# Feed-forward gate-and-up chunks taken in pairs: high-weight products of both, then low-weight products of both

## The chip, the cores and the metric

One core of one Trainium2 chip runs the whole program. The metric is the device time of one execution in microseconds (us), as the median over several executions.

## What is computed

Two DeepNorm layers over 256 tokens of width 1024 in float32. Each layer is a mixer (layer 0: sparse attention and stick-breaking attention; layer 1: block attention) followed by a SwiGLU feed-forward of width 2816. Only the feed-forwards are touched here:

```python
D_FF = -(-8 * D_MODEL // (3 * 256)) * 256      # 2816
def swiglu(x, w_gate, w_up, w_down):
    return (jax.nn.silu(x @ w_gate) * (x @ w_up)) @ w_down

def reference(...):
    for i in range(DEPTH):                     # DEPTH = 2
        ...                                    # mixer and layer norm
        f = swiglu(h, ffn_gate[i], ffn_up[i], ffn_down[i])
        h = layer_norm(DEEPNORM_ALPHA * h + f, ln_ffn_g[i], ln_ffn_b[i])
```

## The kernel before

**Products in parts.** Each float32 weight and activation is split into a high part (rounded to the matmul format fp32r) and a low part (the remainder), and a product is high x high + high x low + low x high. For the gate and up projections the activations lie as `hTs[:, k]`, high and low side by side, 512 columns. `half_hi` runs 8 matmuls of 512 columns, one for each 128 rows of the contraction, with the high weights `whi`; this makes the high x high sum in columns 0 to 255 of a PSUM bank and the high x low sum in columns 256 to 511. `half_lo` adds 8 matmuls of 256 columns with the low weights `wlo` to columns 0 to 255. One **tile** is 128 columns of gate and the same 128 of up: two banks, 16 wide and 16 narrow matmuls.

**The weight stream.** All weights come in chunks of 1 MB, in halves of 512 KB, into two raw buffers (`RAW` = 2). ScalarE (ACT) casts a half to `whi` (`split_hi`, L367), VectorE (DVE) subtracts to get `wlo` (`split_lo`, L737), both into a ring of six chunks (`RING` = 6), four chunks ahead of use (`AHEAD` = 4). The DMA for a half, issued by SyncE (SP, L287), waits until DVE has finished with the same half two chunks earlier. A cast into a ring slot waits until TensorE (PE) has used the chunk that lies in it (`chunk_used`).

**The feed-forward.** A layer has 22 tiles. Tiles 0 and 1 are computed by rows, tiles 2 and 3 one after the other. Then eight **groups** follow, each with three chunks: a down chunk (24 matmuls, L1212, function `out_chunk`) for two earlier tiles, and two gate-and-up chunks. PE writes out the first two groups and loops over the other six; ACT and DVE loop over all eight (`LOOPS` = 4, two groups in each turn). Tiles 20 and 21 come after the last group with no down chunk ahead of them, then the last three down chunks and the layer norm. Banks 4 to 7 accumulate the down products. An even tile has banks 2 and 3, an odd one banks 0 and 1, so a tile's first matmul waits until the tile two before it has been read out (`usum_ready`).

**Reading out a tile** (`ffn_tile`) goes back and forth between ACT and DVE: ACT copies the gate's high x low half (L632), DVE adds (L1016), ACT takes silu (L635) and copies the up half (L637), DVE adds (L1019, after which both banks are free) and multiplies (L1024), ACT casts (L639), DVE subtracts (L1027). The last two make `ahi` and `alo`, which a later down chunk reads.

Each engine runs its instructions in the order in which they are written; semaphores alone couple the engines.

Of the kernel before, what the change touches and what calls it, by code (L numbers as in the profile page):

```python
# [43 lines left out]
AHEAD = 4  # L44
# [16 lines left out]
def build(nc, x, xT, stream, w_uk, w_uv, kv_norm, ln_rows, consts, out):  # L61
    with ExitStack() as ctx:
# [198 lines left out]
        def tile_bank(t):  # L261

            return 2 * ((t + 1) % 2)
# [100 lines left out]
        def _(act):  # L364
# [5 lines left out]
            def split_hi(c, i=0):  # L370

                if c >= RING or not isinstance(i, int):
                    act.wait_ge(chunk_used, c - RING + 1 + RING * i)
                for j in range(2):
                    split_hi_half(c, j, i)
# [249 lines left out]
            def ffn_tile(L, c, t, i=0, more=1, ahi_first=False):  # L625

                n = FT * L + t + 4 * i
                m = n + 1 - 2 * (L + 1)
                if more and not ahi_first:
                    split_hi(c + AHEAD, i)  # L630
                act.wait_ge(gate_done, m)
                nc.scalar.copy(gful[:, t % 2], bank[tile_bank(t)][:, S:2 * S]).then_inc(glo_ready, 1)  # L632
                act.wait_ge(gsum_ready, m)
                act.wait_ge(amul_ready, n - 1)
                nc.scalar.activation(sgate[:, t % 2], gful[:, t % 2], ACT.Silu).then_inc(silu_ready, 1)  # L635
                act.wait_ge(chunk_used, c + 1 + RING * i)
                nc.scalar.copy(uful[:, t % 2], bank[tile_bank(t) + 1][:, S:2 * S]).then_inc(ulo_ready, 1)  # L637
                act.wait_ge(amul_ready, n + 1)
                nc.scalar.copy(ahi[:, FF_SLOT[t], :], aful[:, t % 2]).then_inc(ahi_ready, 1)  # L639
                if more and ahi_first:  # L640
                    split_hi(c + AHEAD, i)

            def ffn(L):


                base = L0_FFN if L == 0 else L1_FFN
                ffn_rows(L, base)
                for t in (2, 3):
                    ffn_tile(L, base + t, t)
                with act.Fori(0, LOOPS) as i:  # L650
                    for j in range(2):
                        c = base + 4 + 3 * j
                        split_hi(c + AHEAD, i)
                        ffn_tile(L, c + 1, 4 + 2 * j, i)
                        ffn_tile(L, c + 2, 5 + 2 * j, i)
                c = base + 4 + RING * LOOPS
                for at in range(3):
                    more = c + at + AHEAD < CHUNKS
                    if at < 2:
                        ffn_tile(L, c + at, 4 + 4 * LOOPS + at, 0, more, at == 1)  # L660
                    elif more:
                        split_hi(c + at + AHEAD)
# [70 lines left out]
        def _(dve):  # L733
# [6 lines left out]
            def split_lo(c, i=0):  # L740

                for j in range(2):
                    split_lo_half(c, j, i)
# [266 lines left out]
            def ffn_tile(L, c, t, i=0, more=1, alo_first=False):  # L1010
                n = FT * L + t + 4 * i
                m = n + 1 - 2 * (L + 1)
                if more and not alo_first:
                    split_lo(c + AHEAD, i)
                dve.wait_ge(glo_ready, m)
                nc.vector.tensor_tensor(gful[:, t % 2], bank[tile_bank(t)][:, 0:S], gful[:, t % 2], ALU.add  # L1016
                                        ).then_inc(gsum_ready, 1)
                dve.wait_ge(ulo_ready, m)
                nc.vector.tensor_tensor(uful[:, t % 2], bank[tile_bank(t) + 1][:, 0:S], uful[:, t % 2], ALU.add  # L1019
                                        ).then_inc(usum_ready, 1)  # L1020
                dve.wait_ge(silu_ready, n + 1)
                dve.wait_ge(usum_ready, m)
                dve.wait_ge(alo_ready, n - 1)
                nc.vector.tensor_tensor(aful[:, t % 2], sgate[:, t % 2], uful[:, t % 2], ALU.mult  # L1024
                                        ).then_inc(amul_ready, 1)
                dve.wait_ge(ahi_ready, n + 1)
                nc.vector.tensor_tensor(alo[:, FF_SLOT[t], :], aful[:, t % 2], ahi[:, FF_SLOT[t], :].bitcast(F32),  # L1027
                                        ALU.subtract).then_inc(alo_ready, 1)
                if more and alo_first:
                    split_lo(c + AHEAD, i)  # L1030

            def ffn(L):


                base = L0_FFN if L == 0 else L1_FFN
                ffn_rows(L, base)
                for t in (2, 3):
                    ffn_tile(L, base + t, t)
                with dve.Fori(0, LOOPS) as i:
                    for j in range(2):  # L1040
                        c = base + 4 + 3 * j
                        split_lo(c + AHEAD, i)
                        ffn_tile(L, c + 1, 4 + 2 * j, i)
                        ffn_tile(L, c + 2, 5 + 2 * j, i)
                c = base + 4 + RING * LOOPS
                for at in range(3):
                    more = c + at + AHEAD < CHUNKS
                    if at < 2:
                        ffn_tile(L, c + at, 4 + 4 * LOOPS + at, 0, more, at == 1)
                    elif more:  # L1050
                        split_lo(c + at + AHEAD)
# [46 lines left out]
        def _(pe):  # L1098
# [4 lines left out]
            def chunk(c, i=0):  # L1103
                pe.wait_ge(wlo_ready, 2 * c + 2 * RING * i)
# [12 lines left out]
            def half_hi(dst, slot, off):  # L1117

                for k in range(KT):
                    mm(dst[:], whi[:, slot, off + k * P:off + (k + 1) * P],  # L1120
                       hTs[:, k].rearrange("p j s -> p (j s)"), start=(k == 0), stop=False)
# [430 lines left out]
                                               aful[:, tile, t * P:(t + 1) * P], ident)  # L1552
                last.then_inc(ff_turned, 1)

            def gate_up(L, c, t, i=0):

                n = FT * L + t + 4 * i
                chunk(c, i)

                pe.wait_ge(usum_ready, n - 1 - 2 * (L + 1))  # L1560
                for half in range(2):
                    half_hi(bank[tile_bank(t) + half], c % RING, half * KT * P)
                half_lo(bank[tile_bank(t)], c % RING, 0).then_inc(gate_done, 1)
                half_lo(bank[tile_bank(t) + 1], c % RING, KT * P).then_inc(chunk_used, 1)

            def down(L, c, p, i=0, start=False):

# [4 lines left out]
            def ffn(L, n):  # L1572
                base = L0_FFN if L == 0 else L1_FFN

                chunk(base + 1)
                two = slice(base % RING, base % RING + 2)
                rows_wide(2 * L + 1, 0, two, bank[0][:], turn=n).then_inc(rows_done, 1)
                rows_wide(2 * L + 1, 1, two, bank[1][:]).then_inc(chunk_used, 2)

                def four_tiles(i, first=False):  # L1580
                    for j in range(2):
                        c = base + 4 + 3 * j
                        down(L, c, j, i, first and j == 0)
                        gate_up(L, c + 1, 4 + 2 * j, i)
                        gate_up(L, c + 2, 5 + 2 * j, i)

                chunk(base + 2)
                for half in range(2):
                    half_hi(bank[tile_bank(2) + half], (base + 2) % RING, half * KT * P)
                turn_rows(L, 0)  # L1590
                turn_rows(L, 1)
                half_lo(bank[tile_bank(2)], (base + 2) % RING, 0).then_inc(gate_done, 1)
                half_lo(bank[tile_bank(2) + 1], (base + 2) % RING, KT * P).then_inc(chunk_used, 1)
                chunk(base + 3)
                for half in range(2):
                    half_hi(bank[tile_bank(3) + half], (base + 3) % RING, half * KT * P)
                half_lo(bank[tile_bank(3)], (base + 3) % RING, 0).then_inc(gate_done, 1)
                half_lo(bank[tile_bank(3) + 1], (base + 3) % RING, KT * P).then_inc(chunk_used, 1)
                four_tiles(0, first=True)
                with pe.Fori(1, LOOPS) as i:  # L1600
                    four_tiles(i)
                c, p = base + 4 + RING * LOOPS, 2 * LOOPS
                gate_up(L, c, 2 * p + 4)
                gate_up(L, c + 1, 2 * p + 5)
                last_out([(c + 2 + j, FF_SLOT[2 * (p + j):2 * (p + j) + 2], FT * L + 2 * (p + j) + 2)
                          for j in range(3)], n + 1)
# [216 lines left out]
```

## Time and profile before

| | |
|---|---|
| median of 3 runs | 600.74 us (600.45 to 601.2) |
| the profiled execution, its own time | 599.96 us |
| its span in the trace | 598.2 us |
| PE matmul busy | 590.4 us (99%) |
| DVE busy | 422.7 us (71%) |
| ACT busy | 342.9 us (57%) |
| bytes read from HBM | 107.94 MB, 182 GB/s over the span |

The span runs from the first to the last instruction of the core. A matmul's recorded duration overlaps the next one's, so what counts for PE is the distance between starts. "Idle before" is time in which an engine stood still ahead of an instruction, with the engine whose event ended it.

### The profile page before, as it was taken

How to read it: one execution, taken by the hardware profiler on the slowest of the kernel's cores; microseconds unless marked ns; L12 is line 12 of the kernel's file. 1: busy time of each engine (PE TensorE's matmuls, PEld its weight loads, DVE VectorE, ACT ScalarE, POOL GpSimd, SP SyncE). 2: the span in 40 equal slices, each digit the busy share in tenths (PEclk: the TensorE clock that was granted, in tenths of full speed). 3: DMA queues.
4: the chain of work that ended last, by engine and by line, in shares of the span. 5: the costliest groups of instructions: out<-in, count | busy, mean ns of one | idle time of the engine just before them, and what ended most of it. 6: DMA issues, size and time to landing. Idle time of an engine off the chain costs nothing.

```text
span 598.2 us, 9656 instructions
## 1 busy us (share of the span) xinstructions
PE 590.4 (99%) x3387; PEld 508.1 (85%) x3387; DVE 422.7 (71%) x694; ACT 342.9 (57%) x644; POOL 27.3 (5%) x49
## 2 busy tenths in 40 slices
PE   9999999999999999999999999999999999999995
PEld 7988887888888888888888898888888888888885
DVE  4699868877776556655887878768677666665637
ACT  5777977466555544554556667636566455555430
POOL 1011111100000000000010000002000000000000
PEclk9999999999999999999999999999999999999999
DMA  8757427376765565564447543662767655555401
GB/s 312 264 178 263 141 70 250 104 253 215 233 219 187 196 204 180 182 205 140 146 139 273 184 141 112 210 202 77 236 217 239 213 189 170 181 188 192 140 1 70
DMA packets 30112, 109.43 MB, mean 183 GB/s; under 512 B 3376, under 2 KB 3376, under 8 KB 29952
## 3 DMA queue, kind: packets, MB, share of 16 engines
q1 hardware_dynamic: 28512, 102.77, 52.2%
q0 software_dynamic: 1568, 6.23, 3.1%
q8 instruction: 21, 0.34, 0.2%
q14 instruction: 11, 0.09, 0.0%
HBM read 107.94 MB, written 1.05 MB: 182 GB/s over the span
## 4 chain that ended last, share of the span: by engine, by line
PE 95%; DMA 2%; DVE 1%; ACT 1%; DVEq 0%; issue 0%; POOL 0%; ACTq 0%; POOLq 0%
PE bank L1212 27%; PE bank L1120 24%; PE bank L1126 13%; PE bank L1647 4%; PE bank L1476 3%; PE bank L1113 2%; PE bank L1190 2%; PE bank L1641 2%; PE bank L1651 2%; DMA raw<-stream_in 2%; PE bank L1166 2%; PE bank L1165 2%; PE bank L1172 2%; PE bank L1307 1%; PE bank L1318 1%; PE bank L1298 1%
## 5 line engine op out<-in xcount | busy, mean ns | idle before, releaser
L737 DVE TENSOR_TENSOR wlo<-raw,whi 128x1024 fp32r<-128x1024 f32 x190 | 225.0, 1223 | 44.0 <-ACT whi L367 43.7
L367 ACT CAST whi<-raw 128x1024 fp32r<-128x1024 f32 x190 | 191.0, 1047 | 16.6 <-DMA raw<-stream_in 15.6
L1120 PE MATMUL bank<-hTs,whi 128*128 128x512 f32 x640 | 152.2, 390 | 0.0
L1120 PEld LDWEIGHTS bank<-hTs,whi 128*128 128x128 f32 x640 | 118.8, 188 | 23.7
L1212 PE MATMUL bank<-whi,oThi 128*128 128x512 f32 x234 | 92.2, 394 | 0.0
L1212 PE MATMUL bank<-whi,oTlo 128*128 128x512 f32 x234 | 91.3, 390 | 0.0
L1212 PE MATMUL bank<-wlo,oThi 128*128 128x512 f32 x234 | 91.1, 389 | 0.0
L1126 PEld LDWEIGHTS bank<-hTs,wlo 128*128 128x128 f32 x640 | 81.9, 191 | 3.0
L1126 PE MATMUL bank<-hTs,wlo 128*128 128x256 f32 x640 | 83.2, 283 | 0.0
L1212 PEld LDWEIGHTS bank<-whi,oThi 128*128 128x128 f32 x234 | 44.0, 188 | 9.3 <-issue 1.0
L1212 PEld LDWEIGHTS bank<-wlo,oThi 128*128 128x128 f32 x234 | 43.9, 188 | 9.4
L1212 PEld LDWEIGHTS bank<-whi,oTlo 128*128 128x128 f32 x234 | 44.0, 188 | 8.0
L632 ACT COPY kT<-bank 128x256 f32<-128x256 f32 x40 | 14.8, 371 | 62.7 <-PE bank L1126 62.7
L1016 DVE TENSOR_TENSOR kT<-bank,kT 128x256 f32<-128x256 f32 x40 | 16.8, 421 | 33.2 <-ACT kT L632 33.1
L639 ACT CAST oThi<-scratch 128x256 fp32r<-128x256 f32 x40 | 16.3, 407 | 41.1 <-DVE scratch L1024 41.1
L1019 DVE TENSOR_TENSOR kT<-bank,kT 128x256 f32<-128x256 f32 x40 | 17.0, 425 | 30.4 <-ACT kT L637 30.4
L635 ACT ACTIVATE scratch<-kT 128x256 f32<-128x256 f32 x40 | 16.7, 418 | 34.1 <-DVE kT L1016 34.1
L1647 PE MATMUL bank<-hTs,whi 128*128 128x512 f32 x128 | 32.6, 395 | 0.0
L1027 DVE TENSOR_TENSOR oTlo<-scratch,oThi 128x256 fp32r<-128x256 f32 x40 | 17.0, 426 | 18.9 <-ACT oThi L639 18.9
L1647 PEld LDWEIGHTS bank<-hTs,whi 128*128 128x128 f32 x128 | 23.0, 189 | 5.1 <-issue 1.0
L1024 DVE TENSOR_TENSOR scratch<-scratch,kT 128x256 f32<-128x256 f32 x40 | 17.0, 426 | 4.4 <-DVE kT L1019 1.5
L1165 PE MATMUL bank<-whi,hTs 128*128 128x512 f32 x48 | 18.8, 392 | 0.0
(192 smaller groups left out, 719.1 us busy)
## 6 DMA issues: line engine op xcount, KB each, us to landing
raw<-stream_in SPq DMA_DIRECT2D x190, 512.0 KB, 5.1
qT<-ln_rows_in POOLq DMA_DIRECT2D x8, 512.0 KB, 5.2
kT<-stream_in SPq DMA_DIRECT2D x2, 512.0 KB, 5.4
v<-xT_in SPq DMA_DIRECT2D x2, 512.0 KB, 5.4
h<-x_in POOLq DMA_DIRECT2D x1, 1024.0 KB, 7.2
out<-h SPq DMA_DIRECT2D x4, 256.0 KB, 2.1
dist<-consts_in POOLq DMA_DIRECT2D x1, 384.0 KB, 3.8
ukv<-w_uk_in POOLq DMA_DIRECT2D x1, 256.0 KB, 7.0
```

The costliest lines, as they stand in the source:

```text
L367: nc.scalar.copy(whi[:, c % RING, j * HW:(j + 1) * HW], raw[:, c % RAW, j * HW:(j + 1) * HW]).then_inc(whi_ready, 1)
L737: nc.vector.tensor_tensor(wlo[:, c % RING, cols], raw[:, c % RAW, cols], whi[:, c % RING, cols].bitcast(F32), ALU.subtract).then_inc(wlo_r ...
L1016: nc.vector.tensor_tensor(gful[:, t % 2], bank[tile_bank(t)][:, 0:S], gful[:, t % 2], ALU.add).then_inc(gsum_ready, 1)
L1019: nc.vector.tensor_tensor(uful[:, t % 2], bank[tile_bank(t) + 1][:, 0:S], uful[:, t % 2], ALU.add).then_inc(usum_ready, 1)
L1024: nc.vector.tensor_tensor(aful[:, t % 2], sgate[:, t % 2], uful[:, t % 2], ALU.mult).then_inc(amul_ready, 1)
L1027: nc.vector.tensor_tensor(alo[:, FF_SLOT[t], :], aful[:, t % 2], ahi[:, FF_SLOT[t], :].bitcast(F32), ALU.subtract).then_inc(alo_ready, 1)
L1120: mm(dst[:], whi[:, slot, off + k * P:off + (k + 1) * P], hTs[:, k].rearrange("p j s -> p (j s)"), start=(k == 0), stop=False)
L1126: last = mm(dst[:, 0:S], wlo[:, slot, off + k * P:off + (k + 1) * P], hThi[:, k, :], start=False, stop=(k == KT - 1))
L1165: mm(dst, hThi[:, k, toks], whi[:, slots, cols], start=(k == 0), stop=False)
L1212: last = mm(bank[4 + 2 * t + a][:], o[:, kts[j], t * P:(t + 1) * P], w[:, c % RING, j * D + a * 512:j * D + (a + 1) * 512], start=(start a ...
L1476: mm(dst[:], whi[:, c % RING, at + k * P:at + (k + 1) * P], hTs[:, k].rearrange("p j s -> p (j s)"), start=(k == 0), stop=False)
L1647: mm(dst[:], whi[:, c % RING, at + k * P:at + (k + 1) * P], hTs[:, k].rearrange("p j s -> p (j s)"), start=(k == 0), stop=False)
```

## The change

The order of work in the eight groups of each layer is changed on three engines. PE runs the 32 wide matmuls of both tiles, then the 32 narrow ones. ACT and DVE convert all three chunks of the group ahead (c+4, c+5, c+6) first and read out both tiles after them, where the conversion of c+5 and c+6 stood in front of one read-out each. Numbers of instructions, buffers and semaphores stay.

```diff
@@ ffn(L), scalar engine (the vector engine has the same edit, with split_lo) @@
                         c = base + 4 + 3 * j
-                        split_hi(c + AHEAD, i)
-                        ffn_tile(L, c + 1, 4 + 2 * j, i)
-                        ffn_tile(L, c + 2, 5 + 2 * j, i)
+                        for at in range(3):
+                            split_hi(c + at + AHEAD, i)
+                        ffn_tile(L, c + 1, 4 + 2 * j, i, 0)
+                        ffn_tile(L, c + 2, 5 + 2 * j, i, 0)
@@ tensor engine @@
-            def gate_up(L, c, t, i=0):
+            def tile_hi(L, c, t, i=0):
                 n = FT * L + t + 4 * i
                 chunk(c, i)
                 pe.wait_ge(usum_ready, n - 1 - 2 * (L + 1))
                 for half in range(2):
                     half_hi(bank[tile_bank(t) + half], c % RING, half * KT * P)
+
+            def tile_lo_part(c, t):
+
                 half_lo(bank[tile_bank(t)], c % RING, 0).then_inc(gate_done, 1)
                 half_lo(bank[tile_bank(t) + 1], c % RING, KT * P).then_inc(chunk_used, 1)
+
+            def gate_up(L, c, t, i=0):
+
+                tile_hi(L, c, t, i)
+                tile_lo_part(c, t)
+
+            def gate_up_pair(L, c, t, i=0):
+
+                for e in range(2):
+                    tile_hi(L, c + e, t + e, i)
+                for e in range(2):
+                    tile_lo_part(c + e, t + e)
@@ four_tiles @@
                         down(L, c, j, i, first and j == 0)
-                        gate_up(L, c + 1, 4 + 2 * j, i)
-                        gate_up(L, c + 2, 5 + 2 * j, i)
+                        gate_up_pair(L, c + 1, 4 + 2 * j, i)
```

On PE, in the first group of layer 0, the end of the down chunk, the two tiles and the start of the next down chunk stood like this before:

```order
L1212 MATMUL bank<-whi,oTlo 128x512
L1212 MATMUL bank<-wlo,oThi 128x512
L1120 MATMUL bank<-hTs,whi 128x512 x16
L1126 MATMUL bank<-hTs,wlo 128x256 x16
L1120 MATMUL bank<-hTs,whi 128x512 x16
L1126 MATMUL bank<-hTs,wlo 128x256 x16
L1212 MATMUL bank<-whi,oThi 128x512
```

At the same place after the change (the lines of the file have moved by two):

```order
L1214 MATMUL bank<-whi,oTlo 128x512
L1214 MATMUL bank<-wlo,oThi 128x512
L1122 MATMUL bank<-hTs,whi 128x512 x32
L1128 MATMUL bank<-hTs,wlo 128x256 x32
L1214 MATMUL bank<-whi,oThi 128x512
```

The second tile's wide matmuls have moved ahead of the first tile's narrow ones; two of the four switches between kinds are gone in each pair.

On ACT, the first group of a turn of the loop, before (L367 is a cast of a half chunk, L632 to L639 the read-out; register instructions step the loop's wait values):

```order
L367 CAST whi<-raw 128x1024 x2
L373 REGISTER_ALU
L366 REGISTER_ALU
L367 CAST whi<-raw 128x1024 x2
L631 ISA
L632 COPY kT<-bank 128x256
L635 ACTIVATE scratch<-kT 128x256
L636 REGISTER_ALU
L637 COPY kT<-bank 128x256
L638 REGISTER_ALU
L639 CAST oThi<-scratch 128x256
L373 REGISTER_ALU
```

After the change the same group begins:

```order
L367 CAST whi<-raw 128x1024 x2
L373 REGISTER_ALU
L366 REGISTER_ALU
L367 CAST whi<-raw 128x1024 x2
L373 REGISTER_ALU
L367 CAST whi<-raw 128x1024 x2
L631 ISA
L632 COPY kT<-bank 128x256
L635 ACTIVATE scratch<-kT 128x256
L636 REGISTER_ALU
L637 COPY kT<-bank 128x256
L638 REGISTER_ALU
```

The third chunk's casts now stand ahead of the first tile's read-out, and nothing but register steps stands between the two read-outs. DVE has the same move.

## Rows read from the trace of the kernel before

**Rows 1.** The page: busy time by engine, and the chain that ended last by engine.
```profile
PE 590.4 (99%) x3387; PEld 508.1 (85%) x3387; DVE 422.7 (71%) x694; ACT 342.9 (57%) x644; POOL 27.3 (5%) x49
...
PE 95%; DMA 2%; DVE 1%; ACT 1%; DVEq 0%; issue 0%; POOL 0%; ACTq 0%; POOLq 0%
```

**Rows 2.** The page's costliest groups: busy us, mean ns, idle before and releaser.
```profile
L367 ACT CAST whi<-raw 128x1024 fp32r<-128x1024 f32 x190 | 191.0, 1047 | 16.6 <-DMA raw<-stream_in 15.6
L1120 PE MATMUL bank<-hTs,whi 128*128 128x512 f32 x640 | 152.2, 390 | 0.0
...
L1126 PEld LDWEIGHTS bank<-hTs,wlo 128*128 128x128 f32 x640 | 81.9, 191 | 3.0
L1126 PE MATMUL bank<-hTs,wlo 128*128 128x256 f32 x640 | 83.2, 283 | 0.0
```

**Rows 3.** The chain in order of time, 150 to 180 us: start, us, what.
```profile
159.91 3.63 PE bank L1120 x16
163.54 1.91 PE bank L1126 x16
165.45 3.65 PE bank L1120 x16
169.10 1.91 PE bank L1126 x16
171.01 5.47 PE bank L1212 x24
```

**Rows 4.** Timeline of PE, layer 1's projections: start, duration, instructions.
```profile
315.40 1.11 PE L1651 MATMUL bank<-hTs,wlo 128*128 128x256 f32 x8
316.35 2.00 PE L1647 MATMUL bank<-hTs,whi 128*128 128x512 f32 x8
318.19 1.11 PE L1651 MATMUL bank<-hTs,wlo 128*128 128x256 f32 x8
```

**Rows 5.** Timeline of PE, two short windows inside one narrow run.
```profile
163.61 0.88 PE L1126 MATMUL bank<-hTs,wlo 128*128 128x256 f32 x6
...
164.57 0.88 PE L1126 MATMUL bank<-hTs,wlo 128*128 128x256 f32 x6
```

**Rows 6.** Timeline of PE, where tile 6's narrow run starts.
```profile
163.37 2.08 PE L1126 MATMUL bank<-hTs,wlo 128*128 128x256 f32 x16
```

**Rows 7.** Timeline of ACT, read-out of tile 6 and the cast behind it.
```profile
164.53 0.37 ACT L632 COPY kT<-bank 128x256 f32<-128x256 f32 x1 [1.28 <-PE bank L1126]
...
167.39 2.00 ACT L367 CAST whi<-raw 128x1024 fp32r<-128x1024 f32 x2
```

**Rows 8.** Timeline of DVE over the same stretch.
```profile
166.10 0.42 DVE L1019 TENSOR_TENSOR kT<-bank,kT 128x256 f32<-128x256 f32 x1 [0.74 <-ACT kT L637]
...
168.47 2.36 DVE L737 TENSOR_TENSOR wlo<-raw,whi 128x1024 fp32r<-128x1024 f32 x2 [0.53 <-ACT whi L367]
```

**Rows 9.** DMA issues at 225.3 to 226.6 us, then at 227.6 to 228.9 us.
```profile
raw<-stream_in SPq DMA_DIRECT2D x2, 512.0 KB, 4.4
...
raw<-stream_in SPq DMA_DIRECT2D x2, 512.0 KB, 6.5
```

**Rows 10.** Timeline, first group of layer 0: PE's tile 4, ACT, DVE.
```profile
143.17 3.79 PE L1120 MATMUL bank<-hTs,whi 128*128 128x512 f32 x16
...
145.28 3.90 ACT L367 CAST whi<-raw 128x1024 fp32r<-128x1024 f32 x4
...
153.36 1.99 ACT L367 CAST whi<-raw 128x1024 fp32r<-128x1024 f32 x2
...
146.36 4.63 DVE L737 TENSOR_TENSOR wlo<-raw,whi 128x1024 fp32r<-128x1024 f32 x4 [0.53 <-ACT whi L367]
```

**Rows 11.** Timeline, last group of layer 0: PE's tiles 18 and 20, ACT.
```profile
259.19 3.79 PE L1120 MATMUL bank<-hTs,whi 128*128 128x512 f32 x16
...
270.29 3.82 PE L1120 MATMUL bank<-hTs,whi 128*128 128x512 f32 x16
...
263.97 0.37 ACT L632 COPY kT<-bank 128x256 f32<-128x256 f32 x1 [4.01 <-PE bank L1126]
```

More of the change, by code:

```diff
@@ L1041, in ffn @@
                         c = base + 4 + 3 * j
-                        split_lo(c + AHEAD, i)
-                        ffn_tile(L, c + 1, 4 + 2 * j, i)
-                        ffn_tile(L, c + 2, 5 + 2 * j, i)
+                        for at in range(3):
+                            split_lo(c + at + AHEAD, i)
+                        ffn_tile(L, c + 1, 4 + 2 * j, i, 0)
+                        ffn_tile(L, c + 2, 5 + 2 * j, i, 0)
                 c = base + 4 + RING * LOOPS
```

## The prediction, made before the changed kernel ran

> **What bounds the kernel now.** I read the page's busy line and its chain first: PE's matmuls are busy 99% of the span, and 95% of the chain that ended last is PE [rows 1]. The costliest groups say whether that is real work: the wide and the narrow matmuls of the tiles stood idle 0.0 us ahead of them over 640 instructions each [rows 2]. The chain in order of time then gives the beat of a group, to be read as five pieces that touch each other: 3.63, 1.91, 3.65, 1.91 and 5.47 us, 16.57 us in all [rows 3]. A wide matmul is 3.63 / 16 = 0.227 us, a narrow one 0.120. The timelines show the other engines with time to spare: before it reads out tile 18, ACT stands still for 4.01 us until PE is there [rows 11]. So the time changes only if PE's own pieces change length, or if a wait of PE that costs nothing now begins to cost.
>
> **What the change does to PE's own pieces.** The instructions are the same 64 in a pair of tiles; only the neighbours change. The chain shows a wide run behind a down chunk (wide matmuls as well) at 3.63 us and a wide run behind a narrow one at 3.65 [rows 3]: a switch from narrow to wide costs 0.02 to 0.03 us. Does the cost grow with the length of the narrow run ahead of it? In layer 1's projections a run of only 8 narrow ones is followed by 8 wide ones that take 318.19 - 316.35 = 1.84 us, where 8 x 0.227 = 1.81 [rows 4]. Again 0.03, so I take it not to grow. The opposite switch gives a little back: 16 narrow ones are 1.91 us where 16 x 0.120 = 1.92 [rows 3], 0.01. A pair loses one switch of each kind, so it gains 0.03 - 0.01 = 0.02 us. Two layers have 16 pairs: 16 x 0.02 = 0.32 us; bounds from the same rows are 0 and 16 x 0.03 = 0.5. No loss from the switches is in the bounds, since none is added.
>
> **The waits on PE.** Call G the time at which ACT can begin to read out the first tile of a pair. Now it is 164.53 - 163.37 = 1.16 us after the narrow run starts (8 gate matmuls and the end of the last) [rows 6, 7]. After the change 32 wide matmuls come first, so G = start of the pair + 7.26 + 1.16 = 8.42. The banks are free after L1019: 166.10 + 0.42 - 164.53 = 2.0 us after G [rows 7, 8]. ACT is held 167.39 - 164.53 = 2.9 us by one read-out, both by 5.8 [rows 7].
>
> *Inside the loop* the pair's banks are next written after this pair (11.1 us) and a down chunk (5.47), at 16.57; the first tile frees them at 10.4. Slack 6.1 us. The second tile is read out from G + 2.9, free at 13.3, and is next needed at 16.57 + 3.63 = 20.2. The down chunk that reads the two tiles comes a group later than the next one; the read-outs end about 0.5 us after ACT's part, at 8.42 + 5.8 + 0.5 = 14.7, and that chunk starts at 11.1 + 16.57 = 27.7.
>
> *At the end of the loop* there is no down chunk. In layer 0 the last pair starts at 259.19 and tile 20 at 270.29 [rows 11]. G becomes 259.19 + 8.42 = 267.61, the banks of tile 18 are free at 269.6, and tile 20's first weights are loaded at about 270.1. That leaves **0.5 us**, where the old order had 263.97 + 2.0 against the same 270.1, 4.1. It is the tightest place of the change, once in each layer. Tile 21 has more: tile 19 is free at 267.61 + 2.9 + 2.0 = 272.5, and is needed 3.65 + 1.91 us after tile 20's start, at 275.9.
>
> **The waits behind which read-outs now stand.** The third chunk's casts are now ahead of both read-outs. Its DMA can start only when DVE is done with the first chunk's halves, since there are two raw buffers. ACT starts the conversions at s = G of the group before + 5.8. DVE starts 1.08 us after ACT and ends the first half 1.22 us later, the second 1.13 after that [rows 7, 8]: issues at s + 2.3 and s + 3.4. The halves issued before that have long landed by then, so the queue is empty then (my reading of the bursts, not a row). Two halves that were issued after a pause, with two more behind them as here, took 4.4 us to land; the two behind took 6.5 [rows 9]. I take 4.4, as the position in the burst is the same: landed by s + 7.8, cast by s + 8.9, which is G of the group before + 14.7. The period is 16.57, so ACT is there **1.9 us before G**. With 6.5 it would be 0.2 us late in each group.
>
> *The first group* starts worse. The third chunk's DMA waits for DVE's first half of 146.36 to 150.99. Its casts ran at 153.36 without a wait for DMA [rows 10], so in the new order they end by 155.4 at the latest, while G is 143.17 + 8.42 = 151.6: up to 3.8 us late. The banks are free at 157.4, and needed at 143.17 + 16.57 = 159.7. PE does not wait, and at 1.9 us a group the lateness is gone after two groups, long before the tight place at the eighth. I take layer 1 to be the same.
>
> The chunks themselves are not at risk: the third is ready at G of the group before + 14.7 + 1.2 for DVE, that is 24.3 us after that pair's start, and the down chunk that uses it starts at 11.1 + 2 x 16.57 = 44.2. DVE's and ACT's totals do not change; what was idle ahead of a read-out becomes idle elsewhere. SP's issues come in bursts of four instead of four and two, with the same bytes. POOL has no part in these stages.
>
> **The sum.** Switches -0.3 us, waits 0. On the profiled execution, 599.96 - 0.3 = 599.6 (span 597.9). That execution lies 0.8 below the median of 600.74, so for a median: 600.74 - 0.3 = **600.4 us**. Runs of one kernel spread over 0.75 us here, so about 0.2% (1.2 us) is the least that this measurement can tell from no change.
>
> **Rivals.**
>
> *ACT too late at the end of the loop: slower.* If the third chunk lands later than s + 2.3 + 4.4, the lateness of the first group is not made up. Break-even of the period is at 4.4 + 1.9 = 6.3 us; to be down from 3.8 to 0.5 us after seven groups, landing must take under 6.3 - 3.3 / 7 = 5.8. That is the point from which it decides. At 6.5 us ACT would be 3.8 + 7 x 0.2 = 5.2 us late at the last group, PE would wait 5.2 - 0.5 = 4.7, twice 9.4: 610 us. For it: 6.5 stands in the rows. Against: those were the third and fourth half of a burst, not the first two [rows 9].
>
> *Long narrow runs slow down: slower.* A narrow matmul's weight load is recorded with 191 ns, over its pitch of 120 [rows 2]. If loads are pulled ahead during the wide matmuls and this store is used up in a narrow run, the second 16 of 32 could go at 191: 16 x 0.071 = 1.1 us a pair, 18 us in all, 619 us. Against it: six matmuls at 163.61 and six at 164.57, early and late in one run, both take 0.88 us [rows 5], and 8 and 16 narrow ones leave the same 0.03 behind. The Trainium skill has such a rule (TensorE: Matmul & The Clock Gate, section Back-to-back issue gap): in a stream of load and matmul pairs the spacing "is set by *both* ops, pipelined through the 64-deep reorder window". By that rule mixing long with short would be worth something and the change could take it away; the trace shows no sign of a store that empties.
>
> *The switches are worth more: faster.* Over 1.2 us would need 0.08 us a pair, three times what the chain shows for one switch. Nothing speaks for it.
>
> *It does not do what it says.* The order of instructions shows 32 wide and 32 narrow ones in a row, so this is excluded.
>
> **Chances.** The forecast (599.8 to 601.6, which is the bounds of the switches, some waiting at the two tight places, and the spread of the runs) 0.88; late ACT 0.06; slow narrow runs 0.02; faster switches 0.03; another cause that costs over 0.2% 0.01. Faster 0.03, within 0.2% 0.88, slower 0.09. The range 599.8 to 601.6 leaves the rivals out, which hold 1.2 in 10 together; its lower end is the 0.5 of the switches and some of the spread below 600.4, its upper end the highest run before, 601.2, and some of the waiting.
>
> **What would show it.** Right: PE's chain has pieces of 7.26, 3.83 and 5.47 us in the groups, PE idle is unchanged, L632 of even tiles starts with ACT waiting for PE for about 1 to 2 us from the third group on, and the first wide matmul of tiles 20 of both layers starts without a gap. Wrong: a gap of PE ahead of tile 20, released by DVE L1019; narrow runs longer than 3.9 us; casts of the third chunk that wait over 5.8 us for their DMA.

## The result: 2.4% slower, and where the time went

The changed kernel took 615.92 us (median of 6, 610.32 to 619.64) against 600.9 us (median of 6, 599.47 to 601.2) for the kernel before: ratio 1.0237, 95% interval 1.0219 to 1.0255. Ratios, here and below, leave out any execution more than 1.5% longer than the shortest of its kernel, here the one of 619.64 us; medians hold them all. The forecast was 600.4. The profiled execution is the shortest of the six, 610.32 us with a span of 608.6 (before: 599.96 and 598.2), so the trace has 10.4 us to explain. The others lost more; they have no trace, and what they lost it on is not shown.

PE's own pieces did what was forecast. The changed kernel's chain in order of time (start, us, what), against [rows 3]:

```profile
204.48 5.47 PE bank L1214 x24
209.94 7.25 PE bank L1122 x32
217.20 3.83 PE bank L1128 x32
```

A group is 16.55 us where it was 16.57. The page of the changed kernel shows another thing: the casts now wait for the DMA for 72.8 us (15.6 before, [rows 2]), PE's wide matmuls have idle time ahead of them where there was none, and PE's granted clock dips in three slices of forty (two of them hold the places shown next; the last is the end of the program).

```profile
PE 594.5 (98%) x3387; PEld 510.9 (84%) x3387; DVE 423.1 (70%) x694; ACT 343.0 (56%) x644; POOL 27.3 (4%) x49
...
PEclk9999999999999999998999999999999999999798
...
L367 ACT CAST whi<-raw 128x1024 fp32r<-128x1024 f32 x190 | 192.5, 1047 | 73.9 <-DMA raw<-stream_in 72.8
L1122 PE MATMUL bank<-hTs,whi 128*128 128x512 f32 x640 | 153.7, 398 | 5.8 <-DVE kT L1020 5.8
```

The timeline of PE shows where. In layer 0 the last pair's narrow run, tile 20's two runs and the start of tile 21's; then the same in layer 1:

```profile
266.69 3.99 PE L1128 MATMUL bank<-hTs,wlo 128*128 128x256 f32 x32
272.77 5.49 PE L1122 MATMUL bank<-hTs,whi 128*128 128x512 f32 x16 [2.08 <-DVE kT L1020]
...
280.01 3.82 PE L1122 MATMUL bank<-hTs,whi 128*128 128x512 f32 x16
...
564.10 3.99 PE L1128 MATMUL bank<-hTs,wlo 128*128 128x256 f32 x32
571.78 6.68 PE L1122 MATMUL bank<-hTs,whi 128*128 128x512 f32 x16 [3.69 <-DVE kT L1020]
```

PE waits ahead of tile 20 for the banks of tile 18 (L1020 is the old L1019), the place that the prediction called the tightest. The 32 narrow matmuls from 266.69 would have been followed at 266.69 + 3.83 = 270.52; tile 20 came at 272.77: 2.25 us. In layer 1 it is 571.78 - 564.10 - 3.83 = 3.85. And the 16 wide matmuls behind each wait take 5.49 and 6.68 us where an undisturbed run has 3.82: 1.67 and 2.86 more. Sum 2.25 + 3.85 + 1.67 + 2.86 = 10.6, less 0.3 for the pairs: 10.3 of the 10.4 us. The windows of those two stretches show the cause of the longer runs in the column of the granted clock (behind the busy times of PE, PEld, DVE, ACT and POOL):

```profile
262.00:270.40 8.40, 8.40 (x53) 7.58 (x52) 5.57 (x6) 4.40 (x6) 0.00 (x0) 1.00 0.72 215
272.77:276.90 4.13, 4.13 (x12) 3.32 (x13) 2.35 (x6) 2.17 (x6) 0.00 (x0) 0.64 0.35 124
...
571.78:577.70 5.92, 5.92 (x14) 4.68 (x15) 3.63 (x8) 3.65 (x7) 0.00 (x0) 0.50 0.00 0
```

0.50 is the lower of PE's two levels, 1.2 GHz, and 0.64 is a mean of stretches at both; the clock was at 1.00 up to the waits.

Why the banks came late is on ACT's timeline, a whole cycle of it from one conversion block to the next:

```profile
161.97 3.90 ACT L367 CAST whi<-raw 128x1024 fp32r<-128x1024 f32 x4
168.22 1.05 ACT L367 CAST whi<-raw 128x1024 fp32r<-128x1024 f32 x1 [2.35 <-DMA raw<-stream_in]
170.47 1.05 ACT L367 CAST whi<-raw 128x1024 fp32r<-128x1024 f32 x1 [1.20 <-DMA raw<-stream_in]
171.43 0.37 ACT L632 COPY kT<-bank 128x256 f32<-128x256 f32 x1
173.15 0.42 ACT L635 ACTIVATE scratch<-kT 128x256 f32<-128x256 f32 x1 [1.35 <-DVE kT L1017]
...
175.14 0.37 ACT L632 COPY kT<-bank 128x256 f32<-128x256 f32 x1
176.06 0.42 ACT L635 ACTIVATE scratch<-kT 128x256 f32<-128x256 f32 x1 [0.55 <-DVE kT L1017]
...
178.16 1.05 ACT L367 CAST whi<-raw 128x1024 fp32r<-128x1024 f32 x1
```

The four casts of two chunks are followed by two waits for the third chunk's halves, 2.35 and 1.20 us, then by two read-outs, none of which waits for PE. 178.16 - 161.97 = 16.19 us. The prediction had 14.7 for this cycle. PE's period is 16.55. ACT was 3.3 us late in the first group (read-out at 155.33, G at 143.57 + 8.42 = 151.99), as forecast (up to 3.8), but it did not catch up: at the eighth group it was still 1.9 late (269.77 against 267.8). In layer 1, which the prediction took to be the same, it was 4.3 us late in the first group and 3.5 in the eighth.

### The profile page after: what moved, and what is told of

It is laid out like the page before. It is cut to its first block, busy times and chain, and to the rows that moved or that the text cites. A ratio compares the mean times of both kernels' runs of the same rounds, so it can differ in the third digit from the quotient of the medians.

```text
span 608.6 us, 9656 instructions
## 1 busy us (share of the span) xinstructions
PE 594.5 (98%) x3387; PEld 510.9 (84%) x3387; DVE 423.1 (70%) x694; ACT 343.0 (56%) x644; POOL 27.3 (4%) x49
## 3 DMA queue, kind: packets, MB, share of 16 engines
HBM read 107.94 MB, written 1.05 MB: 179 GB/s over the span
## 4 chain that ended last, share of the span: by engine, by line
PE 67%; DMA 11%; DVE 9%; ACT 6%; issue 5%; DVEq 0%; ACTq 0%; SPq 0%
PE bank L1214 17%; PE bank L1122 11%; DMA raw<-stream_in 10%; PE bank L1128 5%; PE bank L1663 5%; DVE wlo L738 4%; ACT whi L367 4%; PE bank L1478 3%; PE bank L1667 3%; PE bank L1115 2%; PE bank L1192 2%; PE bank L1657 2%; PE bank L1167 2%; PE bank L1168 2%; PE bank L1174 2%
## 5 line engine op out<-in xcount | busy, mean ns | idle before, releaser
L367 ACT CAST whi<-raw 128x1024 fp32r<-128x1024 f32 x190 | 192.5, 1047 | 73.9 <-DMA raw<-stream_in 72.8
L1122 PEld LDWEIGHTS bank<-hTs,whi 128*128 128x128 f32 x640 | 122.9, 193 | 31.9 <-issue 6.1
L1128 PEld LDWEIGHTS bank<-hTs,wlo 128*128 128x128 f32 x640 | 79.8, 191 | 1.7
L1128 PE MATMUL bank<-hTs,wlo 128*128 128x256 f32 x640 | 80.7, 283 | 0.0
L639 ACT CAST oThi<-scratch 128x256 fp32r<-128x256 f32 x40 | 16.3, 406 | 41.1 <-DVE scratch L1025 41.1
L635 ACT ACTIVATE scratch<-kT 128x256 f32<-128x256 f32 x40 | 16.7, 418 | 38.9 <-DVE kT L1017 38.9
L1020 DVE TENSOR_TENSOR kT<-bank,kT 128x256 f32<-128x256 f32 x40 | 17.0, 425 | 30.4 <-ACT kT L637 30.4
L1663 PEld LDWEIGHTS bank<-hTs,whi 128*128 128x128 f32 x128 | 23.0, 189 | 5.1 <-issue 1.0
L1017 DVE TENSOR_TENSOR kT<-bank,kT 128x256 f32<-128x256 f32 x40 | 16.7, 418 | 6.0 <-ACT kT L632 6.0
L632 ACT COPY kT<-bank 128x256 f32<-128x256 f32 x40 | 14.7, 367 | 8.0 <-PE bank L1128 8.0
```

Of the source, the lines that this page charges most:

```text
L367: nc.scalar.copy(whi[:, c % RING, j * HW:(j + 1) * HW], raw[:, c % RAW, j * HW:(j + 1) * HW]).then_inc(whi_ready, 1)
L1122: mm(dst[:], whi[:, slot, off + k * P:off + (k + 1) * P], hTs[:, k].rearrange("p j s -> p (j s)"), start=(k == 0), stop=False)
L1128: last = mm(dst[:, 0:S], wlo[:, slot, off + k * P:off + (k + 1) * P], hThi[:, k, :], start=False, stop=(k == KT - 1))
L1663: mm(dst[:], whi[:, c % RING, at + k * P:at + (k + 1) * P], hTs[:, k].rearrange("p j s -> p (j s)"), start=(k == 0), stop=False)
```

## The experiments

Theory A: three conversions ahead of two read-outs make a cycle on ACT and DVE that is as long as PE's period, because the third chunk's DMA starts only inside the block; the lateness of the first group stays, slow landings add to it, and it is paid where tile 20 has no down chunk ahead. Rivals: B, PE's own order makes the read-outs late; C, ACT's and DVE's work makes the cycle and the DMA has no part; D, the start has no part, each cycle is too long.

### PE's pairs alone

```diff
-                        for at in range(3):
-                            split_hi(c + at + AHEAD, i)
-                        ffn_tile(L, c + 1, 4 + 2 * j, i, 0)
-                        ffn_tile(L, c + 2, 5 + 2 * j, i, 0)
+                        split_hi(c + AHEAD, i)
+                        ffn_tile(L, c + 1, 4 + 2 * j, i)
+                        ffn_tile(L, c + 2, 5 + 2 * j, i)
```

The same on DVE; PE keeps the changed order.

> Only PE's order is changed; ACT and DVE keep the order of before (two conversions, read-out, conversion, read-out). Theory A (the loss comes from the read-outs standing behind three conversions, whose cycle of about 16.4 us cannot make up the first group's lateness): no gap ahead of tile 20 in either layer, clock 1.00, time 600.4 to 601.2, ratio 0.999 to 1.001. Theory B (the loss comes from PE's order: the gate is done 3.6 us later after a pair's start, so the read-outs end too late for the banks): gaps of 2 us or more ahead of tile 20 remain, time 606 or more.

599.48 us, ratio 0.9993 (0.9984 to 1.0002), mean granted clock of the profiled execution 0.999. The chain has the pieces of the changed kernel and nothing between them, and nothing waits:

```profile
160.00 7.25 PE bank L1120 x32
167.25 3.83 PE bank L1126 x32
171.08 5.47 PE bank L1212 x24
```

ACT waits for PE again ahead of tile 18, and tile 20 starts on time (timeline of ACT, then of PE, last group of layer 0):

```profile
267.56 0.37 ACT L632 COPY kT<-bank 128x256 f32<-128x256 f32 x1 [3.99 <-PE bank L1126]
...
270.24 3.82 PE L1120 MATMUL bank<-hTs,whi 128*128 128x512 f32 x16
```

So G was at 267.6 as computed, and 0.5 us of slack is enough when ACT is on time. B has fallen.

### The conversions alone

The edit above the other way round, on the kernel of before.

> Only ACT's and DVE's order is changed; PE keeps the order of before. Theory A: ACT's cycle is held by its own chain and the DMA, not by PE, so the read-out of tile 18 comes at about the same time, the gaps ahead of tile 20 remain at 2 to 4 us in each layer and the clock falls behind them: ratio 1.01 to 1.03. Theory B: no gap, ratio 1.00.

617.28 us, ratio 1.0315 (1.028 to 1.0351), more than the whole change and above the expected range. PE's timeline in layer 0:

```profile
268.58 2.07 PE L1128 MATMUL bank<-hTs,wlo 128*128 128x256 f32 x16
276.05 4.18 PE L1122 MATMUL bank<-hTs,whi 128*128 128x512 f32 x9 [5.40 <-DVE kT L1020]
```

All of the loss is in ACT's and DVE's order. B is out a second time. The waits are longer than the expected 2 to 4 us (4.83 us in layer 1): from the first group's read-out to the eighth's, ACT's cycle is here (275.09 - 158.16) / 7 = 16.7 us in layer 0 and 16.9 in layer 1, longer than PE's period. Why it is longer than in the changed kernel is not shown.

### The third chunk's load made small

```diff
+            THIRD = [b + 10 + 3 * g for b in (L0_FFN, L1_FFN) for g in range(8)]
...
-                            sp.dma_start(raw[:, s, half[j]], stream[RAW * i + s][:, half[j]]
+                        cols = slice(j * HW, j * HW + (32 if c in THIRD else HW))
+                        sp.dma_start(raw[:, c % RAW, cols], stream[c][:, cols]
```

SP's loop is written out for this.

> The changed kernel, where the third chunk of each group is loaded with 32 of 1024 columns a half only (the rest of the weights is stale, so this leaves out part of the load; all instructions on the engines are the same). Theory A: the casts of the third chunk wait for DMA for under 0.5 us, ACT's cycle falls to 13.5 to 14.5 us, the first group's lateness of over 3 us is gone within two groups, no gap ahead of tile 20, time 600 to 601. Theory C (DVE's and ACT's own work makes the cycle, the DMA is no cause): cycle over 16 us and gaps as in the changed kernel, time 608 or more.

599.61 us, ratio 0.9991 (0.9982 to 1.0000), no gap ahead of tile 20. ACT's timeline, from one block to the next:

```profile
159.53 6.16 ACT L368 CAST whi<-raw 128x1024 fp32r<-128x1024 f32 x6
168.71 0.37 ACT L633 COPY kT<-bank 128x256 f32<-128x256 f32 x1 [3.01 <-PE bank L1129]
...
174.58 3.90 ACT L368 CAST whi<-raw 128x1024 fp32r<-128x1024 f32 x4
```

The same instructions on ACT and DVE, with six casts in a row and 3.01 us left over before PE is there in the second group already. C has fallen: without the third chunk's landing the cycle is 174.58 - 159.53 - 3.01 = 12.0 us, less than the 13.5 to 14.5 expected. Less data is in flight here too, which this run does not separate.

### The third conversion behind the read-outs

```diff
-                        for at in range(3):
+                        for at in range(2):
                             split_hi(c + at + AHEAD, i)
                         ffn_tile(L, c + 1, 4 + 2 * j, i, 0)
                         ffn_tile(L, c + 2, 5 + 2 * j, i, 0)
+                        split_hi(c + 2 + AHEAD, i)
```

> PE as in the changed kernel; ACT and DVE convert two chunks, read out both tiles, then convert the third. In a steady loop this is the same cyclic order (three conversions, two read-outs), but the first group's read-outs are not behind the third chunk. Theory A with its part on the start (the lateness is made in the first group and kept, as the cycle is about equal to the period): read-outs start within 0.5 us of PE in the first group, no or small gaps ahead of tile 20, ratio 0.999 to 1.003. Theory D (the cycle is longer than the period, and the lateness is made group by group): gaps of over 1 us in both layers, ratio over 1.008.

603.95 us, ratio 1.0064 (1.005 to 1.0078): between the two. The first group's read-outs were on time and the wait in layer 0 was down to 0.28 us, so about three quarters of the loss hung on the start. But in layer 1 lateness built up from nothing. ACT was on time in the third group; the cycles that end with the read-outs of the fourth, seventh and eighth took 17.3, 17.6 and 17.1 us, and it was 0.7, 1.6 and 2.1 us late there. ACT's timeline has the eighth's waits for the third chunk's halves:

```profile
561.08 1.05 ACT L367 CAST whi<-raw 128x1024 fp32r<-128x1024 f32 x1 [2.60 <-DMA raw<-stream_in]
563.71 1.05 ACT L367 CAST whi<-raw 128x1024 fp32r<-128x1024 f32 x1 [1.58 <-DMA raw<-stream_in]
564.66 0.37 ACT L632 COPY kT<-bank 128x256 f32<-128x256 f32 x1
```

PE's timeline at tile 20 of that layer:

```profile
567.66 5.50 PE L1124 MATMUL bank<-hTs,whi 128*128 128x512 f32 x16 [2.27 <-DVE kT L1021]
```

D is partly right: a cycle that is on average as long as the period has single cycles that are longer, and two in a row made most of this wait.

### The changed kernel again, as a base

> The changed kernel again, beside the next three on the same chip, as their base. Ratio 1.018 to 1.03; gaps of 2 to 6 us ahead of tile 20 in both layers, of different length in each execution, as the landing of the third chunk decides.

612.96 us, ratio 1.0226 (1.0184 to 1.0268). Its profiled execution has waits of 2.90 and 4.17 us at the two places.

### Zero matmuls in the gap

```diff
+                for _ in range(16):
+                    mm(bank[4][:], zeros[:, 2 * P:3 * P], zeros[:], start=False, stop=False, skip_group_check=True)
                 gate_up(L, c, 2 * p + 4)
```

> The changed kernel with 16 wide matmuls of zero weights (they add zero to a down bank) ahead of tile 20 in each layer, 16 x 0.227 = 3.63 us of work in the place where PE stood still. If the clock's fall behind the gap is a cost of its own (about 1.9 and 3.1 us in the profiled run of the changed kernel), the filled kernel keeps a clock of 1.00 there, the wide matmuls behind it go at 0.227 us, and the time is that of before + 2 x the larger of 3.63 and ACT's lateness: 607 to 611, under the changed kernel on the same chip in spite of the added work. If the clock is no cost of its own, the time is not under that of the changed kernel.

611.63 us, ratio 1.0192 (1.0141 to 1.0243): not to be told from the base. In the profiled execution layer 0 lost nothing beyond the added work, but in layer 1 ACT was later than 3.63 us, a wait of 2.00 us remained and the clock fell behind it all the same (5.47 us for 16 wide matmuls). As a test of the clock's price it is inconclusive.

### The old order in the last group only

```diff
-                with act.Fori(0, LOOPS) as i:
+                with act.Fori(0, LOOPS - 1) as i:
...
+                i = LOOPS - 1
...
+                    else:
+                        split_hi(c + AHEAD, i)
+                        ffn_tile(L, c + 1, 4 + 2 * j, i)
+                        ffn_tile(L, c + 2, 5 + 2 * j, i)
```

> The changed kernel with the old order on ACT and DVE in the last group of each layer alone (two conversions, read-out of tile 18, third conversion, read-out of tile 19). Theory A: only the last group has a tight place, so all the lateness of the seven groups before is harmless: tile 18 is read out 4 to 5 us earlier, no gap ahead of tile 20 or one under 0.5 us, ratio 0.999 to 1.004. Rival (lateness also costs inside the loop, or tile 19 is late for tile 21): ratio over 1.01.

600.62 us, ratio 1.0008 (0.9994 to 1.0023). ACT read out tile 18 on time even though it was late in the group before (timeline of ACT; 257.87 is the read-out of tile 16, the next L632 but one that of tile 18):

```profile
257.87 0.37 ACT L632 COPY kT<-bank 128x256 f32<-128x256 f32 x1
...
269.49 0.37 ACT L632 COPY kT<-bank 128x256 f32<-128x256 f32 x1 [1.08 <-PE bank L1152]
```

So the lateness is paid at the end of the loops, as long as it is small enough. In this execution it was not: after slow landings (one second half took 7.5 us in layer 0, one 7.1 in layer 1) ACT was 5.7 us late in the fourth group of layer 0 and 6.1 in the sixth of layer 1, more than the slack inside the loop (6.1 us less the 0.9 by which a late bank comes later still, see below), and PE waited there too. Its timeline in layer 0:

```profile
211.19 7.55 PE L1146 MATMUL bank<-hTs,whi 128*128 128x512 f32 x32 [0.28 <-DVE kT L1032]
```

In layer 1 it is the same line at 539.26, with a wait of 0.67 us.

### Zero matmuls ahead of the first group

The same 16 matmuls, on bank 7, ahead of `four_tiles(0, first=True)`.

> The changed kernel with the same 16 zero matmuls (3.63 us) ahead of the first group of each layer, nothing at the end. Theory A with the start as source of the lateness: PE comes 3.6 us later to every group, ACT's and DVE's chain does not, so the lateness is gone, no gap ahead of tile 20 or a small one, clock 1.00; time of before + 7.3 - 0.3 = 607 to 609, 5 us or more under the changed kernel in spite of the added work. Rival D (cycle longer than the period): the gaps stay at 1 us or more in both layers, time 614 or more.

609.38 us, ratio 1.0136 (1.0115 to 1.0156). 600.14 x 1.0136 = 608.3; less 7.3 us of added work that is 601.0, where the changed kernel beside it has 600.14 x 1.0226 = 613.7. In three executions of five, starting PE 3.6 us later took away nearly all of the loss. The other two took 619.33 and 621.44 us, 12 and 14 us over the kernel of before and the added work, as rival D expected. The profile is of the first of these; the three others have none. In it ACT was on time until a half took long to land, and ended a cycle 2 us late for good.

```profile
222.35 0.37 ACT L632 COPY kT<-bank 128x256 f32<-128x256 f32 x1 [0.54 <-PE bank L1128]
...
240.21 1.05 ACT L367 CAST whi<-raw 128x1024 fp32r<-128x1024 f32 x1 [4.42 <-DMA raw<-stream_in]
241.16 0.37 ACT L632 COPY kT<-bank 128x256 f32<-128x256 f32 x1
```

241.16 - 222.35 = 18.81 us for one cycle. PE then waited 1.98 us ahead of tile 20. Layer 1 had two such cycles, and a wait of 5.37 us. So the start is one source of lateness and a slow landing another; the order makes up neither.

### Little in flight beside the third chunk

The edit of the small third chunk, for the chunk behind it in the stream (`b + 8 + 3 * g`, g from 1 to 7).

> The changed kernel, with 32 of 1024 columns a half loaded for the chunk that follows the third in the stream (the first to be converted in the next group), so that little is in flight beside the third chunk, which is loaded in full. Stale weights: this leaves out part of the load. If the third chunk's second half lands late because the next chunk's two halves share the queue, it now lands 3.8 to 4.2 us after its issue (4 to 6 now), a conversion block takes 8.5 to 9 us in place of 8.6 to 10.7, ACT's cycle falls under 15.6, the lateness is made up and there is no gap ahead of tile 20: ratio 0.998 to 1.002. If the landing is the same fixed latency however much is in flight: second half still 4.5 us and more, gaps remain, ratio over 1.01.

602.08 us, ratio 1.0028 (1.0014 to 1.0042). Most of the loss is gone, but not for the reason given: the profiled execution still waits 2.54 and 1.78 us for the third chunk in the last block, and PE 2.0 us in layer 1.

```profile
559.41 1.05 ACT L368 CAST whi<-raw 128x1024 fp32r<-128x1024 f32 x1 [2.54 <-DMA raw<-stream_in]
562.23 1.05 ACT L368 CAST whi<-raw 128x1024 fp32r<-128x1024 f32 x1 [1.78 <-DMA raw<-stream_in]
563.19 0.37 ACT L633 COPY kT<-bank 128x256 f32<-128x256 f32 x1
```

The landing of the second half is hardly better with an emptier queue: 4.0 to 5.8 us after issue, 4.8 in the middle, where the profiled execution of the changed kernel has 3.9 to 6.0 and 5.1. In layer 0 that was enough: the cycle was (218.18 - 155.01) / 4 = 15.8 us and ACT was back on time in the sixth group. In layer 1 it was 16.5, and of 4.3 us of lateness 3.9 were left at the end. Neither expectation holds as written, and why most of the ten executions lost so little is not shown.

### The price of a gap by itself

On the kernel of before, ahead of tile 20, a wait for tile 19's last step; and the same with 13 zero matmuls ahead of it.

```diff
                 c, p = base + 4 + RING * LOOPS, 2 * LOOPS
+                pe.wait_ge(alo_ready, FT * L + 20)
```

> The kernel of before with one more wait: PE waits ahead of tile 20 in each layer until tile 19's last step is done, 273.2 us in layer 0 where tile 20 started at 270.3, so a gap of 3.0 to 3.2 us in each layer that has nothing to do with DMA or lateness. If a gap costs its own length alone: 2 x 3 = 6 us, ratio 1.010. If PE's clock falls behind it each time (8 to 14 wide matmuls at 0.427 in place of 0.227 us): 9 to 11 us, ratio 1.015 to 1.019.

> The same added wait with 13 wide matmuls of zero weights ahead of it (2.95 us), so that PE stands still for about 0.2 us only. Time lost is 2 x 3.1 = 6 to 7 us in both views; if the clock is a cost of its own, this kernel is faster than the one without the filler by 3 to 4 us although it does more work; if not, the two are the same.

608.04 us, ratio 1.0124 (1.0108 to 1.0139), and 607.05 us, ratio 1.0112 (1.0096 to 1.0127). PE's timeline at tile 20 of layer 0, without the zero matmuls:

```profile
273.57 5.54 PE L1120 MATMUL bank<-hTs,whi 128*128 128x512 f32 x16 [2.78 <-DVE oTlo L1027]
```

The same place with the zero matmuls (L1604):

```profile
271.77 3.14 PE L1604 MATMUL bank<-zeros 128*128 128x512 f32 x13
274.75 3.90 PE L1120 MATMUL bank<-hTs,whi 128*128 128x512 f32 x16
```

5.54 against 3.90 us: the clock fell behind a wait of 2.8 us and stayed up when PE had work, as expected. But that execution is the longest of its four (609.14; the others 607.27 to 608.45), and over all of them the fall costs 600.6 x 0.0012 = 0.7 us where 3 to 4 were expected, with intervals that overlap. The mean granted clock goes with the times: 0.993 at 609.14 us, 0.996 at 608.45 and 607.63, 0.999 at 607.27, as high as in any execution of the kernel before. So the clock's fall is real in single executions and, by these clocks, does not happen in all.

### PE's pairs once more

> PE's pairs with the old order on ACT and DVE, a second time, to narrow the interval: 16 pairs x 0.02 us = 0.3 us, ratio 0.9995, interval within 0.0010 of it on either side. A ratio under 0.998 would say that the switches between wide and narrow are worth over three times what the chain shows.

599.59 us, ratio 0.9989 (0.998 to 0.9998). Both intervals hold the 0.9995 of the forecast for the switches; the first holds 1 as well, the second just leaves it out. Of the versions that leave nothing out this has the lowest times: 0.6 and 1.0 us under the kernel of before in its two measurements, of which 0.3 are explained.

## Why the prediction was wrong, step by step

**Right.** PE's pieces (7.25 and 3.83 us, 16.55 a group), the switches at 0.02 us a pair, G, the place (tile 20, 0.5 us of slack, wait for L1019), and layer 0's lateness in the first group (3.3 of up to 3.8 us; layer 1's, 4.3, is over that bound). Nothing inside the loop was tight in this execution; with 5.7 us of lateness it was. Of the three signs of being wrong the gap ahead of tile 20 showed. The narrow runs stayed under 3.9 us, and the third chunk's second half took over 5.8 us to land in 5 of 16 groups, so that sign gave little warning.

**The step that failed** is under "The waits behind which read-outs now stand": "landed by s + 7.8, cast by s + 8.9 [...] so ACT is there 1.9 us before G", and with it "at 1.9 us a group the lateness is gone after two groups". The cycle was summed as 8.9 + 5.8 = 14.7 us. Measured, from block to block in layer 0, are (260.13 - 145.68) / 7 = 16.35, and from read-out to read-out in layer 1 (568.78 - 453.65) / 7 = 16.45. The mechanism was right and two terms of this sum were too small:

- *The conversion block*, taken as 8.9: 171.52 - 161.97 = 9.55 us in the cycle shown, 8.6 to 10.7 over all. The 4.4 us in [rows 9] is the middle of two landings, and the block ends with the later one, 4.7. Taken one by one, issues of the changed kernel at 164.45 and at 165.58 us, then the second of [rows 9]'s burst in the kernel before:

```profile
raw<-stream_in SPq DMA_DIRECT2D x1, 512.0 KB, 3.7
...
raw<-stream_in SPq DMA_DIRECT2D x1, 512.0 KB, 4.9
...
raw<-stream_in SPq DMA_DIRECT2D x1, 512.0 KB, 4.7
```

  That burst was also an unlucky choice. These loops of the kernel before have 16 bursts of four halves; in two of them, this one and another, the second half landed after 4.7 us, in the others after 5.0 to 6.6, and the middle of all is 5.4. The prediction's own sum with 5.4 gives s + 3.4 + 5.4 + 1.05 = s + 9.9, 1.0 more, so this much could be had from the trace before.
- *The read-outs*: 178.16 - 171.43 = 6.7 us, of which about 0.9 is the first one's silu, which waits 1.35 us in place of 0.5, since DVE is still busy with the third chunk's low part when ACT has done its casts. I took both read-outs, 5.8, from a place where DVE was free [rows 7, 8].

A catch-up of 0.2 us a group in place of 1.9 left 1.9 us at the last group of layer 0, and one of 0.1 left 3.5 in layer 1. The bank comes 0.9 us later than G + 2.0 for the same reason as above, and the slack is 0.5: 1.9 + 0.9 - 0.5 = 2.3, measured 2.25. In layer 1 3.5 + 0.9 - 0.5 = 3.9, measured 3.85.

**The rival** "ACT too late at the end of the loop" named the mechanism, the place and, with 610 us, the size of the profiled execution. It got 0.06, because its point of decision (a landing of 5.8 us) rested on the same sum. With the measured terms the second half, issued 165.58 - 161.97 = 3.6 us into the block, has to land within 16.55 - 6.7 - 3.6 - 1.05 = 5.2 us for the cycle to equal the period, and within 5.2 - 3.3 / 7 = 4.7 to be on time at the eighth group. In the profiled execution it took 3.9 to 6.0 us, 5.1 in the middle.

**Not in the forecast at all** was the clock behind a wait: 4.5 of the 10.4 us in the profiled execution. In the other five the mean granted clock was no higher (0.985 to 0.988, against 0.989 in the profiled one and 0.999 before), so it was a cost there too; how much is not shown.

The other two rivals are out: the narrow matmuls keep 0.120 us through a run of 32 (3.83 us), so the used-up store of weight loads does not show. The Trainium skill (TensorE: Matmul & The Clock Gate, section Back-to-back issue gap) says that weight loads and matmuls together set the spacing, pipelined through a reorder window; no run here shows a cost from that when long and short matmuls are grouped. And the switches are not worth 0.08 us a pair: the middle values of the two ratios of PE's pairs alone give 0.4 and 0.7 us over 16 pairs, 0.03 and 0.04 each.

**Open**: why the second of two halves takes about a microsecond more to land than the first when little else is in flight, and what makes a single one take several more. A third raw buffer was not tried, so whether it cures the order is open.

## What to carry to other kernels

Before an engine's work is bunched, add up one full cycle of the chain in its new order, each wait taken from a place where the partner engine is as busy as it will be, and each landing by the last piece that ends the block; then set it against the period of the bound engine. Here the two were within 0.2 us: the chain hardly caught up, and any lateness, from the start or from one slow transfer, travelled to the first place without slack. With two prefetch buffers two conversions ran in a row; the third waited for a DMA that had been issued only inside the block. And take a wait from many cases of the trace, not from one: the one chosen here had, of 16, one of the two shortest.

Reordering the engine that is 99% busy cost nothing while its partners' order stayed: the gain and the loss came from different parts of one change, and one run for each part told them apart.

## What the runs showed of the hardware

PE's clock fell to the lower level behind waits of 2.08 us (5.49 us for the next 16 wide matmuls) and 3.69 us (6.68 us). In the second run of the changed kernel 16 wide matmuls behind a wait of 2.90 us took 3.91 us, which is the full clock's time (3.90 us behind the zero matmuls above; timeline of PE):

```profile
273.23 3.91 PE L1122 MATMUL bank<-hTs,whi 128*128 128x512 f32 x16 [2.90 <-DVE kT L1020]
```

The profiled executions have thirteen waits of 1.98 to 5.40 us ahead of tile 20; behind this one and the one of 1.98 us the clock stayed up, behind the eleven others it fell. The length of the wait does not tell which: one of 2.00 us cost the clock, the one of 2.90 did not. Where the clock fell it cost 1.6 to 2.9 us on top. The Trainium skill (TensorE: Matmul & The Clock Gate, Part 1: The HAM clock gate) describes these two levels, 1.2 and 2.4 GHz; the 0.50 in the windows agrees.
